# Where the last value unit's matmuls stand in the delta stage: behind two Gram groups, with a gate unit's in their old place

## What is computed

```python
def c_mixer(h, w_in, conv_w, a_log, dt_bias, head_gain, w_out):
    qkv, gate, b, a = _split(h @ w_in, C_SIZES)          # 3072, 1024, 8, 8 columns
    qkv = jax.nn.silu(short_conv(qkv, conv_w))           # 4 taps along the tokens
    q, k, v = ...                                        # 8 heads of 128 each; q, k of length 1
    beta, log_alpha = sigmoid(b), -exp(a_log) * softplus(a + dt_bias)
    o = gated_deltanet(q, k, v, beta, log_alpha)
    o = rmsnorm(o, head_gain) * silu(gate)
    return o @ w_out

def gated_deltanet(q, k, v, beta, log_alpha):
    g = cumsum(log_alpha) in each chunk
    decay = exp(g[i] - g[j]) for j <= i, else 0
    lower = beta * (k @ k.T) * decay, strictly lower     # the "Gram" matrices
    u, w = (I + lower)^-1 @ [beta * v, beta * exp(g) * k]
    attn = (q @ k.T) * decay
    ... the two or four chunks in order, with a state S
```

## Time and profile before

| | us |
|---|---|
| median of 3 runs | 1328.74 |
| lowest and highest | 1327.57, 1329.91 |
| the profiled execution, its device time | 1329.45 |
| the profiled execution, its span | 1327.6 |
| TensorE busy in it | 1271.8 |

### The profile page before, as it was taken

How to read it: one execution, slowest core, us unless ns; L and a number is a source line. 1 busy time by engine, 2 the same in 40 slices (tenths; PEclk the granted TensorE clock), 3 DMA queues, 4 the chain that set the end, 5 groups by cost and what they waited for, 6 DMA issues and landing times.

```text
span 1327.6 us, 22040 instructions
## 1 busy us (share of the span) xinstructions
PE 1271.8 (96%) x9160; PEld 1152.9 (87%) x9160; DVE 792.4 (60%) x1163; ACT 707.6 (53%) x1118; POOL 128.3 (10%) x146
## 2 busy tenths in 40 slices
PE   6999999999999989999999999998999999999997
PEld 6988899998888877888999888987998888999886
DVE  5786678885456555645555446786645635655444
ACT  6767666664476534644655335554355634655433
POOL 6000001110000000000111000105600000111000
PEclk9999999999999998999999999998999999999999
DMA  9433465555544523543555555532203534465550
GB/s 335 161 117 107 143 191 187 176 180 196 188 138 175 190 69 137 175 143 112 169 182 189 191 177 159 183 120 92 92 8 111 190 128 139 149 189 190 191 191 32
DMA packets 141430, 205.52 MB, mean 155 GB/s; under 512 B 3730, under 2 KB 118802, under 8 KB 141330
## 3 DMA queue, kind: packets, MB, share of 16 engines
q1 hardware_dynamic: 141330, 204.11, 46.5%
HBM read 203.05 MB, written 1.05 MB: 154 GB/s over the span
## 4 chain that ended last, share of the span: by engine, by line
PE 84%; DVE 7%; ACT 5%; issue 2%; POOL 1%; DMA 1%; SPq 0%; DVEq 0%; ACTq 0%; POOLq 0%
PE ps L303 40%; PE ps L365 27%; PE ps L383 5%; PE ps L2080 2%; DVE weights_lo L282 2%; PE ps L1705 1%; ACT weights_hi L279 1%; PE ps L2142 1%; PE ps L1727 1%; PE ps L487 1%; POOL arena L2368 1%; DVE split_arena L518 1%; ACT normed L904 1%; DMA weights<-in_w_in 1%; PE ps L755 0%
## 5 line engine op out<-in xcount | busy, mean ns | idle before, releaser
L282 DVE TENSOR_TENSOR weights_lo<-weights,weights_hi 128x1024 fp32r<-128x1024 f32 x379 | 471.4, 1255 | 253.5 <-ACT weights_hi L279 251.3
L303 PE MATMUL ps<-split_arena,weights_hi 128*128 128x256 f32 x3056 | 561.8, 286 | 8.5 <-DVE split_arena L518 6.8
L279 ACT ACTIVATE weights_hi<-weights 128x1024 fp32r<-128x1024 f32 x379 | 396.7, 1056 | 274.3 <-PE ps L365 182.7
L303 PEld LDWEIGHTS ps<-split_arena,weights_hi 128*128 128x128 f32 x3056 | 479.3, 193 | 17.2 <-issue 12.0
L303 PE MATMUL ps<-split_arena,weights_lo 128*128 128x256 f32 x1528 | 433.4, 284 | 0.0
L303 PEld LDWEIGHTS ps<-split_arena,weights_lo 128*128 128x128 f32 x1528 | 294.4, 193 | 0.0
L365 PE MATMUL ps<-weights_hi,split_arena 128*128 128x512 f32 x992 | 272.7, 392 | 2.4 <-ACTq L1877 1.6
L365 PEld LDWEIGHTS ps<-weights_hi,split_arena 128*128 128x128 f32 x992 | 184.5, 188 | 41.7 <-issue 2.9
L365 PE MATMUL ps<-weights_lo,split_arena 128*128 128x512 f32 x496 | 153.7, 390 | 0.0
L365 PEld LDWEIGHTS ps<-weights_lo,split_arena 128*128 128x128 f32 x496 | 93.1, 188 | 19.7
L1885 POOL TENSOR_TENSOR normed<-normed 128x512 f32<-128x512 f32 x32 | 34.1, 1065 | 502.0 <-ACTq L1877 502.0
(11 more groups left out here) (364 smaller groups left out, 1321.3 us busy)
## 6 DMA issues: line engine op xcount, KB each, us to landing
weights<-in_mlp_w SPq DMA_DIRECT2D x64, 1024.0 KB, 5.3
weights<-in_w_up SPq DMA_DIRECT2D x22, 1024.0 KB, 5.1
weights<-in_c_w_in SPq DMA_DIRECT2D x16, 1024.0 KB, 5.4
weights<-in_w_in SPq DMA_DIRECT2D x14, 1024.0 KB, 6.3
weights<-in_ab_w_in SPq DMA_DIRECT2D x12, 1024.0 KB, 5.3
weights<-in_w_down SPq DMA_DIRECT2D x11, 1024.0 KB, 4.9
weights<-in_xa_wv SPq DMA_DIRECT2D x8, 1024.0 KB, 4.9
weights<-in_xa_wq SPq DMA_DIRECT2D x8, 1024.0 KB, 5.2
```

Source lines behind the costliest of these rows:

```text
L279: act.activation(h, r, ACT.Copy).then_inc(s_hi, 1)
L282: dve.tensor_tensor(l, r, h.bitcast(F32), ALU.subtract).then_inc(s_lo, 1)
L303: mm = pe.matmul(o, w[:, k, :], x[:, k, :], start=(k == 0 and i == 0), stop=(k == DC - 1 and i == 2))
```

## The change

In the weight stream the second of gate's units and the last of v's change places, so parts GP0 and GP0+1 now belong to gate unit 1 (stage `c_gate1`) and GP0+2 and GP0+3 to value unit 11 (stage `c_v1`). TensorE computes gate unit 1 where unit 11 was, its second part behind `products(0)`, and unit 11 behind `products(2)` and `products(3)`, into bank 0 in place of bank 3. ScalarE and VectorE move unit 11's taps, convolution and SiLU behind the fourth group, and convert parts GP0+3 to GP0+5 one by one between the groups. The waits follow. `c_pool` is not edited.

```diff
-            cols("c_v", "c_w_in", [2560, 2816])
-            cols("c_gate", "c_w_in", range(3328, 4096, 256))
+            cols("c_v", "c_w_in", [2560])
+            cols("c_gate1", "c_w_in", [3328])
+            cols("c_v1", "c_w_in", [2816])
+            cols("c_gate", "c_w_in", range(3584, 4096, 256))
...
-        GP0 = first_part[first_unit["c_gate"]] - 2
+        GP0 = first_part[first_unit["c_gate"]] - 4
...
+        def conv_bank(u):
+            return PS[:, G + (u % 4 if u < 11 else 0), :]
...
-            free(11)
-            cols_part(first_unit["c_v"] + 1, 0, HT, G + 3)
+            pe.wait_ge(named("c_conv"), 10)
+            cols_part(first_unit["c_gate1"], 0, HT, 1)
             gate_columns()
-            cols_part(first_unit["c_v"] + 1, 1, HT, G + 3)
...
                 elif n == 2:
-                    pe.wait_ge(named("c_conv"), NCU)
+                    pe.wait_ge(named("c_conv"), 11)
...
                 elif f == 0:
-                    pe.wait_ge(named("c_conv"), 11 - u)
-                cols_part(first_unit["c_gate"] + u - 1, f, HT, u % 2)
+                    pe.wait_ge(named("c_conv"), NCU)
+                cols_part(first_unit["c_gate"] + u - 2, f, HT, u % 2)
...
-                pe.wait_ge(named("c_silu"), NCU)
+                pe.wait_ge(named("c_silu"), 11 if gi < 2 else NCU)
...
             products(0)
+            cols_part(first_unit["c_gate1"], 1, HT, 1)
             products(1)
             products(2)
-            gate_part(2)
+            cols_part(first_unit["c_v1"], 0, HT, 0)
             products(3)
-            gate_part(3)
+            cols_part(first_unit["c_v1"], 1, HT, 0)
...
-            for u in range(NCU):
+            def taps(u):
+                cols_done(act, *unit_at(u))
+                for f in range(2):
+                    t = TILE[u] + f
+                    ins = act.activation(CC[:, u % 4, f, :], conv_bank(u)[:, f * T:(f + 1) * T], ACT.Copy,
+                                         scale=cconv_cols[:, t, 3:4])
+                ins.then_inc(named("c_tap"), 1)
+
+            for u in range(NCU - 1):
...
-            silu(NCU - 1)
+            silu(NCU - 2)
             act.preload_act_table_set(EXP_LN)
...
-            decays(0)
-            decays(1)
-            decays(2)
-            split(act, GP0 + 5)
-            decays(3)
             act.wait_ge(named("c_row"), 3)
             act.activation(GE[:, :, :], GCB[:, :, 32:72], ACT.Exp).then_inc(named("c_log"), 1)
             act.activation(GX[:, 1, :], GX[:, 0, :], ACT.Exp).then_inc(named("c_log"), 1)
             act.wait_ge(named("c_log"), 6)
+            decays(0)
+            gate_evac(1)
+            split(act, GP0 + 3)
+            decays(1)
+            split(act, GP0 + 4)
+            decays(2)
+            split(act, GP0 + 5)
+            decays(3)
+            taps(NCU - 1)
             split(act, GP0 + 6)
-            gate_evac(1)
+            silu(NCU - 1)
+            act.preload_act_table_set(EXP_LN)
             decays(4)
             query_decay(0)
             split(act, GP0 + 7)
...
             dve.sem_inc(named("c_row"), 1)
-            conv(NCU - 1)
...
             exponents(0)
+            split(dve, GP0 + 3)
+            decayed(0)
             exponents(1)
-            decayed(0)
+            split(dve, GP0 + 4)
+            decayed(1)
             exponents(2)
-            decayed(1)
+            split(dve, GP0 + 5)
+            decayed(2)
             exponents(3)
-            decayed(2)
             decayed(3)
-            split(dve, GP0 + 5)
+            conv(NCU - 1)
             split(dve, GP0 + 6)
```

More of the change, by code:

```diff
@@ L1968, in unit_at @@
         def unit_at(u):
-            return ("c_qkv", u) if u < 10 else ("c_v", u - 10)
+            return ("c_qkv", u) if u < 10 else (("c_v", "c_v1")[u - 10], 0)
         def heads_at(n):
@@ L2230, in c_act @@
                                    ACT.Copy).then_inc(named("c_ge"), 1)
[L2231 to L2236, removed]
+                taps(u)
                 if u:
@@ L2253, in gate_evac @@
             def gate_evac(u):
-                act.wait_ge(s_used, GP0 + 2 * u + 2)
+                act.wait_ge(s_used, GP0 + 2 * u + (2 if u > 1 else 0))
                 act.activation(SGT[:, 2 * u:2 * u + 2, :], PS[:, u % 2, :].rearrange("p (c n) -> p c n", c=2),
@@ L2409, in conv @@
                         ins = dve.scalar_tensor_tensor(
-                            out=CC[:, u % 4, f, lag:T], in0=PS[:, G + u % 4, f * T:(f + 1) * T - lag],
+                            out=CC[:, u % 4, f, lag:T], in0=conv_bank(u)[:, f * T:(f + 1) * T - lag],
                             scalar=cconv_cols[:, TILE[u] + f, tap:tap + 1], in1=CC[:, u % 4, f, lag:T], op0=ALU.mult,
```

## The result

| | before | changed |
|---|---|---|
| median us | 1329.33 (4 runs, 1327.57 to 1330.22) | 1340.1 (4 runs, 1336.43 to 1341.58) |
| profiled execution, span | 1327.6 | 1339.3 |

The ratio of the changed kernel's time to the one before is 1.0079, 95% interval 1.0054 to 1.0103: slower by 0.8%, some 10.5 us. The forecast was 1340.0.

What follows compares the result with a forecast made beforehand. The prediction took the stretch before blocks(6) to be bound by ScalarE and VectorE leading to GpSimd's masks, held by unit 11's SiLU. 11.5 later plus 0 for clock on 1328.74 gave 1340.2, taken as 1340.0; range 1337 to 1343.

Steps and rivals of the forecast that it cites:

- Nothing on the path is removed: On TensorE, the same parts and products run in another order, hidden behind its wait for GpSimd: cost 0.
- Step 1: Until group 0 is through: ScalarE's gate_evac(1) waits for the gate's second part, ahead of GP0+3's conversion; exponents(1) at 907.65.
- Step 2: Groups 1 and 2, each now with a conversion in it: 4.8 us a group, exponents(3) at 917.25.
- Step 3: Group 3 and unit 11's convolution and SiLU, its table load hidden: first GpSimd mask starts at 924.6.
- Step 4: GpSimd's six masks, undisturbed by VectorE conversions, take 7.96 us; TensorE starts blocks(6) at 932.6.
- the other bound: For the six masks on GpSimd: 9.7 us if they take as long as before, 13.3 in all.
- The sum: Delay of blocks(6) plus clock: 11.5 + 0 = 11.5 us, on the median of before 1340.2, taken as 1340.0.
- The clock: TensorE's half speed behind the wait costs 4.0 now; a longer wait adds 0, bounds a gain of 2.0 and 1.5 upward.
- Rival B: Masks held by unit 11's SiLU, but full clock returns 4 us after TensorE's restart: 1338.2, or 1337; chance 0.12.
- Rival C: GpSimd's six masks all run at their long price, 2.15 each, 5.3 more: 1345.5; chance 0.05.
- Rival D: Group 0's early start reaches the masks, removing TensorE's 5.8 us wait and up to 4.0 of clock: 1319 to 1323; chance 0.02.

Runs made afterwards that it cites:

- the third experiment: Changed kernel with gate_evac(1) on ScalarE moved from behind decays(0) to behind decays(3): 1341.06 us (1 run).
- the second experiment: Changed kernel with conversions of GP0+4, GP0+5 and GP0+6 taken out from between the groups, put behind unit 11's SiLU (ScalarE) and convolution (VectorE): 1336.38 us, ratio 1.0063.
- Both fills: Unused matmuls keep TensorE busy in its wait for the masks: 136 added to the changed kernel, 1336.41 us; 38 added to the kernel before, 1325.65 us.
- the kernel with all three edits: Changed kernel; only masked(1,1) waits for unit 11's SiLU, no conversions between groups, gate_evac(1) behind the fourth group: 1326.39 us, ratio 0.9971.
- the first three experiments: Changed kernel with one edit each: only masked(1,1) waits for unit 11's SiLU, 1331.97 us; the second experiment, 1336.38; the third experiment, 1341.06.
- the last kernel: Against the kernel with all three edits: GP0+4 converted between third and fourth group, VectorE's later conversions one part behind: 1324.81 us, ratio 0.9958.

## Why the prediction was right

- **Nothing on the path is removed.** TensorE's records come to 1271.7 us busy against 1271.8: its new order costs nothing.
- **Step 1.** `exponents(1)` at 907.36 (907.97 less the 0.61 by which the stage starts later), forecast 907.65. From the start of `products(0)` (899.73) to that of `products(1)` (904.32) it is 4.59 and not 1.76 + 3.07 = 4.83, which is most of the 0.3. That the gate's part holds it is shown by the third experiment.
- **Step 2.** 4.75 a group, forecast 4.8. The second experiment shows what the three later conversions cost: 5.0 on the first mask.
- **Step 3.** The first mask at 924.17 on the same scale, forecast 924.6. The table load for SiLU (920.93 to 922.21) lay under the convolution, which ended at 924.05.
- **Step 4.** 7.92 for six masks, forecast 7.96 from undisturbed ones. The second experiment shows the other bound at work: three beside conversions take 2.6 more.
- **The sum.** 11.5 forecast, 11.0 in the trace, 10.5 (7.2 to 13.7) by the ratio of the runs. The mechanism is right, but that 1340.0 met the median of 1340.1 so closely is partly luck: the steps are 0.5 too long together, and the four runs of the changed kernel lie 5 us apart.
- **The clock.** 0 forecast, 3.55 - 3.86 = -0.3 measured, and the rest of the span takes this back (from the end of the second blocks to the end of the span it is 397.2 and was 396.8). Both fills show the clock's price by itself. Rival B's early recovery didn't come: by the rows below of the changed kernel (us, PE busy, granted clock, DMA share, GB/s) TensorE restarts in the first of them and is back at full clock only within the last, 8 us later. A low clock of under 4 us does exist, in the kernel with all three edits, but there it fell only behind the restart.

```profile
932.00:933.00 1.00, 0.30 (x6) 0.50 0.00 0
939.00:940.00 1.00, 1.00 (x13) 0.50 0.00 0
940.00:941.00 1.00, 1.00 (x29) 0.64 0.00 0
```

- **Rival C** (long masks) needed VectorE's two-input work beside the masks; the second experiment made that happen, and three of the six then lengthened; in the changed kernel none did. **Rival D** rested on a GpSimd that doesn't wait for unit 11 and groups that don't wait for conversions. Both had to be written in, and then it came: the first mask of the kernel with all three edits starts at 907.8 on the common scale, and the times are 1326.4 and 1324.8. D's price of 1319 to 1323 was too good. It took the whole wait of 5.8 away, and 2.29 and 1.62 of it stayed; and unit 11 then holds masked(1,1), and through it the second blocks, for another 1.75 and 1.69.

## What to carry to other kernels

Before work is moved later, look at every engine's waits for its result, also at those that the edit doesn't touch: a counter that waits for "all twelve" turns into the critical wait when the twelfth moves. Wait for the unit whose buffer is really reused. And a conversion that costs nothing in an idle stretch costs nearly its full time on both engines when it is queued between two steps of a chain that hand over to each other: a group took 4.75 with it, and 2.66 without it in the second experiment.

## What the runs showed of the hardware

- Behind waits of 5.8, 8.3, 15.0, 16.0 and 17.3 us TensorE restarted at the low clock, 1.2 GHz. From `blocks(6)` to the end of the next blocks it then took 9.71 (the kernel before), 9.91, 9.96, 9.48 (the first three experiments) and 9.40 (the changed kernel), against 5.85 at full clock: a price of 3.55 to 4.1 us that did not grow with the wait.
- In the kernel with all three edits the clock stood at full when TensorE restarted behind waits of 2.29 and 1.75 us, and fell within 0.4 us of the restart. The price was smaller, 1.3 and 1.55 on 64 matmuls. Behind waits of 1.62 and 1.69 in the last kernel it didn't fall. What decides between these cases is not shown.
- The Trainium skill ("SBUF — State Buffer", section "Who interferes with whom") calls the contention of the shared ports an exclusive lock. In the records both sides become longer: in the second experiment three masks of 1.26 took 2.13 each, and the three conversions beside them 5.75 together, where two take 2.36 undisturbed. A mask and a conversion, 1.26 + 1.18 = 2.44 if one waited for the whole of the other, passed every 2.2 us. So they ran nearly one after the other, which is close to a lock; whether the ports change hands within an instruction, these records don't tell.
